# Spreading one modulation pair's one-column products over the k steps of a projection block

## The chip, the cores and the metric

The kernel runs on one core of a Trainium2 chip. The metric is the time of one execution on the device, in microseconds (us); lower is better.

## The reference

Two transformer blocks of one family run one after the other on 512 latent tokens and 256 context tokens of width 1024. What bears on this case is the first layer of the first block. From two condition vectors it makes six modulation vectors each, it norms and modulates the tokens, and it projects them to the inputs of four mixers:

```python
m = jnp.dot(jax.nn.silu(cond), w_mod) + b_mod          # 1024 -> 6 * 1024, for c and for c_ctx
h = modulate(rms_norm(x, norm1_g[l]), sh1, sc1)
q, k, v, u_pool, a_conv, b_conv = jnp.split(h @ w_in[l], SPLITS, axis=-1)
q = apply_rope(rms_norm(q.reshape(...), q_g)); k = apply_rope(rms_norm(k.reshape(...), k_g))
u = a_conv * jax.nn.sigmoid(b_conv)                     # 31 taps, then a layer norm over 256 channels
y = silu(layer_norm(depthwise_conv(u) + dw_b, ln_g, ln_b))
```

Attention, a pooling mixer, the output projection and a gated feed-forward follow. The second layer and the second block are of the same kind.

## The kernel before, in words

It is one program of hand-ordered instruction streams, one for each engine, that meet at semaphores. Activations lie with channels on the partitions and 768 tokens along the free axis. Weights are split into a high and a low part, so that each product of a weight tile with the activations is three matrix products: high with high, high with low, low with high. SyncE (SP) loads raw weights, ScalarE (ACT) writes `w_hi`, and GpSimd (POOL) or VectorE (DVE) writes `w_lo` = raw minus `w_hi`. Work is numbered in blocks `n` of mostly 256 output channels; two PSUM slots and two weight slots alternate. `gemm_done` counts the blocks that TensorE (PE) has finished, `lo_ready` the blocks whose `w_lo` is written, `psum_free` the evictions.

**The first layer's input projection** is ten blocks, b = 0 to 9. Blocks 0 and 1 make the convolution's input, 2 and 3 the pool's, 4 to 7 the queries and keys. Blocks 8 and 9 make the values with tokens on the partitions (`products_nat`): six token tiles of eight k steps each, 48 k steps of three products with 256 columns (line 2998). Between the k steps of block 8 stand small products that belong elsewhere, by the table `key_sums`: step number 0 to 11 each carries one product of the third group of head sums (the squares' sums over a head, two columns, line 3054), 12 to 23 one product of the convolution's sums of squares (one column, line 3108), 24 to 28 none, 29 to 40 one product of the fourth group of head sums, 41 to 47 none. The last of these four groups opens a chain: ACT takes the root (`roots(3)`, line 2113), DVE inverts it (`inverse(3)`, line 2590) and rotates the last keys (`rotate(3)`, lines 2596 to 2598), then multiplies the convolution's result (line 2660, semaphore `c_yn`), and PE's turn of the first key root (`turn_root(4)`, line 3128), which stands between the first and the second token tile of block 9, waits for that. Before it, at block 8's end, PE turns the convolution's root (`conv_root_turned`, line 760), which waits for the root of the fourth head sums.

**Modulation pairs.** A pair is 512 columns of `w_mod`, two rings of 256. DVE multiplies each weight row by the condition and accumulates (`pair_steps`, line 2496, 16 steps for a pair with both conditions), once for the latents in `mod_w` and once for the context in `mod_ctx`. PE then sums over the partitions with eight one-column products (`pair_sum`, line 2846), four blocks of 128 columns for each of the two conditions. The eight results are copied out of PSUM into `modc` (`pair_save`), which raises `mod_saved` by two. `pair_in_block` says behind which block's products a pair's sums stand. The pair of this case is (0, 6), the seventh of the first layer; its sums stand behind block 7. Its place in PSUM is shared in time with the convolution's sums and the fourth head sums, so these wait for `mod_saved`. SP loads the next pair's weights, (0, 7), only after `mod_saved` of (0, 6), and its queue then holds the swap of the last keys for `rotate(3)` (`load_swap`, line 635).

On DVE the order around block 7 is: convolution taps, four steps of pair (0, 6), the convolution's centring (line 2641, semaphore `c_yc`), the other twelve steps, `w_lo` of block 8 (`own_lo(8)`, line 2615), then the inverses and rotations. On ACT it is: `w_hi` of block 9 (line 1929) once block 7 is done, the save of the pair, block 7's squares and copy out of PSUM (lines 2207 and 2210), the root of the third head sums, the convolution's root (line 2236). `late_pair` is a semaphore that PE raises for a pair with sums in the middle of a block of the output projection.

## Time and profile before

| what | value |
|---|---|
| median of 3 runs | 2481.96 us (2480.01 to 2485.34) |
| profiled execution, its own time | 2481.36 us |
| its span in the profile | 2479.6 us |
| mean granted clock of TensorE | 0.982 |
| PE busy | 2393.6 us, 97% of the span |
| DVE, ACT, POOL busy | 1342.5, 818.2, 848.1 us |
| chain that ended last | PE 85%, DVE 10%, ACT 3% |
| queue of SP's loads | 238.41 MB, 31.6% of the 16 engines |

The span runs from the first to the last instruction seen; the execution's own time has 1.8 us more around it. A granted clock of 1.00 is TensorE's upper level, 2.4 GHz, and 0.50 its lower, 1.2 GHz. A matrix product's duration in a row of the timeline contains its way through the array, so that rows overlap; the pace is read from the starts. In a timeline a small f32 product appears as two rows merged into "x2".

### The profile page before, as it was taken

To read this page: it belongs to the slowest core of one execution; us is meant where nothing else is said; L and a number is where in the kernel's file an instruction comes from. 1 tells how busy PE (TensorE), PEld (TensorE's weight loads), DVE (VectorE), ACT (ScalarE), POOL (GpSimd) and SP (SyncE) were. 2 spreads that over 40 slices of the span, in tenths; PEclk is the share of its full clock that TensorE was granted. 3 is DMA by queue.
4 is the path that set the end of the run, shared out by engine and by line. 5 is a ranking of instruction groups with operands and counts; after the bars stand their busy time and mean duration, and the time that the engine had idled before them with its cause. 6 is when DMAs were issued, how large, how long until landed. Compare 5 with 4: busy or idle time off the path is not lost.

```text
span 2479.6 us, 31918 instructions
## 1 busy us (share of the span) xinstructions
PE 2393.6 (97%) x13433; PEld 2015.6 (81%) x13433; DVE 1342.5 (54%) x1823; ACT 818.2 (33%) x1195; POOL 848.1 (34%) x615
## 2 busy tenths in 40 slices
PE   7999889999999999998899999999999989999998
PEld 3889778888888888788788778778988678887877
DVE  3986677645543543697767755655563445211114
ACT  2322672321211112435742222235353454222223
POOL 1005103234333333205034554544453003444452
PEclk9997899999999999999999999999999999999999
DMA  8332112324342442223033545632113102233231
GB/s 259 119 102 87 35 35 70 101 95 120 113 141 90 138 131 89 73 86 104 1 103 106 166 146 168 196 102 85 52 35 102 34 1 69 82 99 100 83 96 68
DMA packets 309231, 240.58 MB, mean 97 GB/s; under 512 B 10692, under 2 KB 304831, under 8 KB 309087
## 3 DMA queue, kind: packets, MB, share of 16 engines
q1 hardware_dynamic: 308674, 238.41, 31.6%
q8 instruction: 106, 1.74, 0.3%
q14 instruction: 37, 0.30, 0.0%
q10 hardware_dynamic: 414, 0.13, 0.0%
HBM read 232.22 MB, written 2.10 MB: 95 GB/s over the span
## 4 chain that ended last, share of the span: by engine, by line
PE 85%; DVE 10%; ACT 3%; issue 1%; POOL 1%; DMA 1%; SPq 0%; DVEq 0%; ACTq 0%
PE ps L2893 54%; PE ps L2933 6%; PE ps L1339 5%; PE ps L2998 3%; PE ps L1098 2%; PE ps L1359 1%; DVE mod_w L2496 1%; DVE h_lo L2400 1%; PE ps L835 1%; PE ps L753 1%; PE ps L2811 1%; DVE small L1223 1%; DVE xg L2415 1%; POOL w_lo L1816 1%; PE ps L808 1%
## 5 line engine op out<-in xcount | busy, mean ns | idle before, releaser
L1816 POOL TENSOR_TENSOR w_lo<-raw,w_hi 128x512 fp32r<-128x512 f32 (+1 forms) x488 | 694.8, 1453 | 1260.1 <-ACT w_hi L1929 1260.1
L2893 PE MATMUL ps<-h_hi,w_hi 128*128 128x512 f32 (+1 forms) x1704 | 549.7, 368 | 3.3 <-DVE h_lo L2400 1.5
L2893 PE MATMUL ps<-h_hi,w_lo 128*128 128x512 f32 (+1 forms) x1704 | 541.5, 363 | 0.0
L2893 PE MATMUL ps<-h_lo,w_hi 128*128 128x512 f32 (+1 forms) x1704 | 541.2, 363 | 0.0
L1929 ACT ACTIVATE w_hi<-raw 128x2048 fp32r<-128x2048 f32 (+4 forms) x162 | 259.1, 1599 | 431.7 <-PE ps L2893 317.3
L2893 PEld LDWEIGHTS ps<-h_hi,w_hi 128*128 128x128 f32 x1704 | 287.0, 188 | 60.2 <-POOL w_lo L1816 3.6
L2893 PEld LDWEIGHTS ps<-h_hi,w_lo 128*128 128x128 f32 x1704 | 286.9, 188 | 56.0
L2893 PEld LDWEIGHTS ps<-h_lo,w_hi 128*128 128x128 f32 x1704 | 287.0, 188 | 54.8 <-issue 0.2
L2278 ACT ACTIVATE xg<-ps 128x512 f32<-128x512 f32 (+1 forms) x66 | 44.2, 670 | 636.0 <-PE ps L2893 388.0
L2496 DVE SCALAR_TENSOR_TENSOR mod_w<-mod_w,cond 128x512 f32<-128x512 f32 x217 | 224.2, 1033 | 3.4
L2893 PE MATMUL ps<-hid_hi,w_hi 128*128 128x512 f32 x632 | 210.0, 371 | 0.0
L2893 PE MATMUL ps<-hid_lo,w_hi 128*128 128x512 f32 x632 | 209.0, 370 | 0.0
L2893 PE MATMUL ps<-hid_hi,w_lo 128*128 128x512 f32 x632 | 208.8, 369 | 0.0
L2526 DVE SCALAR_TENSOR_TENSOR x<-ps,modc,x 128x512 f32<-128x512 f32 (+1 forms) x132 | 83.0, 680 | 182.5 <-PE ps L2893 182.5
L2760 DVE TENSOR_TENSOR sq<-xg,ps 128x512 f32<-128x512 f32 (+1 forms) x66 | 51.0, 773 | 237.4 <-ACT xg L2278 237.3
L2763 DVE TENSOR_TENSOR hid_lo<-sq,hid_hi 128x512 fp32r<-128x512 f32 (+1 forms) x66 | 88.0, 1333 | 76.9 <-ACT hid_hi L2282 76.9
L2893 PEld LDWEIGHTS ps<-hid_hi,w_lo 128*128 128x128 f32 x632 | 108.8, 189 | 22.2
L2893 PEld LDWEIGHTS ps<-hid_lo,w_hi 128*128 128x128 f32 x632 | 108.8, 189 | 21.9
L2893 PEld LDWEIGHTS ps<-hid_hi,w_hi 128*128 128x128 f32 x632 | 108.9, 189 | 21.7
L1260 DVE SCALAR_TENSOR_TENSOR conv_acc<-u_conv,col_b,conv_acc 128x783 f32<-128x783 f32 (+1 forms) x120 | 107.2, 893 | 3.9
L2496 DVE SCALAR_TENSOR_TENSOR mod_ctx<-mod_w,cond,mod_ctx 128x512 f32<-128x512 f32 x105 | 102.3, 975 | 0.0
L2933 PE MATMUL ps<-h_hi,w_hi 128*128 128x256 f32 (+1 forms) x288 | 86.7, 301 | 1.6 <-DVE h_lo L2400 1.6
(424 smaller groups left out, 4079.6 us busy)
## 6 DMA issues: line engine op xcount, KB each, us to landing
mod_w<-in_w_mod SPq DMA_DIRECT2D x72, 1024.0 KB, 8.2
raw<-in_w_ffn_in SPq DMA_DIRECT2D x88, 512.0 KB, 5.2
raw<-in_w_in SPq DMA_DIRECT2D x54, 512.0 KB, 4.9
raw<-in_w_ffn_out SPq DMA_DIRECT2D x48, 384.0 KB, 3.7
raw<-in_w_out SPq DMA_DIRECT2D x24, 512.0 KB, 4.7
raw<-in_w_gate SPq DMA_DIRECT2D x22, 512.0 KB, 4.0
raw<-in_w_up SPq DMA_DIRECT2D x22, 512.0 KB, 5.3
raw<-in_w_down SPq DMA_DIRECT2D x24, 384.0 KB, 3.4
```

The source lines that it names most:

```text
L1098: ins = pe.matmul(ps[:, PV2_AT:PV2_AT + 256], values(us[u]["k0"] // P + k, us[u]["h"]), probs_t[:, k, 256 * (j % 2):256 * (j % 2) + 256], ...
L1260: ins = dve.scalar_tensor_tensor(acc, frm, w, acc, ALU.mult, ALU.add)
L1339: ins = pe.matmul(ps[:, at:at + tw], weight, v[:, k, t0:t0 + tw], start=(k == 0 and r == 0), stop=(k == KD - 1 and r == 2))
L1816: ins = pool.tensor_tensor(lo[:, at:end], raw[:, s, at:end], hi[:, at:end].bitcast(F32), ALU.subtract)
L1929: ins = act.activation(to[:, at], raw[:, n % 2, at], ACT.Copy)
L2496: ins = dve.scalar_tensor_tensor(to, w, by, to if step >= chains else mod_bias[:, :, :], ALU.mult, ALU.add)
L2526: ins = dve.scalar_tensor_tensor(xt, ps[:, at:at + tw], modc[:, l % 2, chunk + 2 * b + t, c:c + 1], xt, ALU.mult, ALU.add)
L2760: dve.tensor_tensor(ffn_tile(ffn_h[:, s, 0:T], n, T), ffn_tile(ffn_sg[:, s, 0:T], n, T), ffn_columns(n, 1, T), ALU.mult).then_inc(psum_fre ...
L2763: dve.tensor_tensor(hid_lo[:, i, 0:T], ffn_h[:, s, 0:T], hid_hi[:, i, 0:T].bitcast(F32), ALU.subtract).then_inc(f_lo, 1)
L2893: ins = pe.matmul(ps[0:m, at:at + tw], weight(part, k, cols), v[:, held[k] if held else k, t0:t0 + tw], start=(at_k == 0 and j == 0 and no ...
L2933: ins = pe.matmul(ps[:, at:at + tw], w[:, k, P * tile:P * tile + P], v[:, held[k] if held else k, t0:t0 + tw], start=(at_k == 0 and j == 0 ...
L2998: ins = pe.matmul(ps[:, first + width * t:first + width * (t + 1)], v[:, k, rows], w[:, k, :], start=(k == 0 and j == 0), stop=(k == KD - ...
```

## The change

The eight one-column products of pair (0, 6) no longer stand behind block 7. They go one by one into k steps 12 to 19 of block 8, in their old order and with the old operands. The convolution's sums of squares move from steps 12 to 23 to steps 20 to 31, the fourth head sums from 29 to 40 to steps 35 to 46; of the free steps in between there are three instead of five, and behind the last head sum one instead of seven. ACT saves the pair after the root of the third head sums instead of ahead of block 7's eviction, and waits for `late_pair` there. The later reader of `late_pair` waits for 2 instead of 1. Block 7 ends with its own last product, and the wait for `c_yc` behind it is gone (the third head sums already wait for it). The second layer keeps its steps but for the fourth head sums, which begin three free steps behind the convolution's sums instead of five.

```diff
@@ ACT
-                        pair_save(lambda to, frm: act.activation(to, frm, ACT.Copy), n)
+                        if n != base_in[0] + 7:
+                            pair_save(lambda to, frm: act.activation(to, frm, ACT.Copy), n)
...
                         if b == 7:
                             roots(2)
+                            if l == 0:
+                                act.wait_ge(late_pair, 1)
+                                pair_save(lambda to, frm: act.activation(to, frm, ACT.Copy), n)
@@ DVE
                 if pair:
-                    dve.wait_ge(late_pair, 1)
+                    dve.wait_ge(late_pair, 2)
@@ PE
+            def pair_product(m, at, number):
+
+                ring, e, part = number // 4, number // 2 % 2, number % 2
+                if number == 0:
+                    pe.wait_ge(mod_mul, pair_ops[pair_at[m] + 1])
+                ins = pe.matmul(ps[:, at + number:at + number + 1], mod_part(ring, part, True)[:, P * e:P * e + P], ones[:, 0:1],
+                                start=True, stop=True)
+                if number == 7:
+                    ins.then_inc(late_pair, 1)
...
-                if n not in pair_in_block:
+                if n not in pair_in_block or n == base_in[0] + 7:
                     return None
...
                         number, conv, key = KD * t + k, 2 * T // P, 2 * TOK // P
+                        pair = key if l else key + 8
                         if number < key:
                             head_sum(2, number)
-                        elif number < key + conv:
-                            conv_square_sum(number - key)
-                        elif number >= key + conv + 5:
-                            head_sum(3, number - key - conv - 5)
+                        elif number < pair:
+                            pair_product((0, 6), pair_columns(base_in[0] + 7), number - key)
+                        elif number < pair + conv:
+                            conv_square_sum(number - pair)
+                        elif number >= pair + conv + 3:
+                            head_sum(3, number - pair - conv - 3)
...
-                            pair = then
-
-                            def pair_after_conv():
-
-                                pe.wait_ge(c_yc, 2 * l + 2)
-                                return pair()
-
                             products(n, KD, in_width(l, b), spans(TOK if b >= 6 else T), h_hi, h_lo, kr,
-                                     pair_after_conv if then and b == 7 else then, None, in_at, None,
+                                     then, None, in_at, None,
```

The first place is PE at the seam of blocks 7 and 8 (`mod_w` and `mod_ctx` hold the pair's sums, `w_hi`, `w_lo` the weights, `h_hi`, `h_lo` the activations, `qk_sq` the squares of the queries and keys). Before:

```order
779 L2893 MATMUL ps<-h_hi,w_lo 128x256
780 L2846 MATMUL ps<-const,mod_w 128x1 [waits mod_mul,c_yc]
781 L2846 MATMUL ps<-const,mod_ctx 128x1
...
787 L2846 MATMUL ps<-const,mod_ctx 128x1
788 L2998 MATMUL ps<-w_hi,h_hi 128x256 [waits psum_free0,lo_ready]
789 L2998 MATMUL ps<-w_hi,h_lo 128x256
790 L2998 MATMUL ps<-w_lo,h_hi 128x256
791 L3054 MATMUL ps<-const,qk_sq 128x2 [waits p_std,c_yc,p_sq]
```

And with the change:

```order
779 L2907 MATMUL ps<-h_hi,w_lo 128x256
780 L3012 MATMUL ps<-w_hi,h_hi 128x256 [waits psum_free0,lo_ready]
781 L3012 MATMUL ps<-w_hi,h_lo 128x256
782 L3012 MATMUL ps<-w_lo,h_hi 128x256
783 L3068 MATMUL ps<-const,qk_sq 128x2 [waits p_std,c_yc,p_sq]
```

The eight products are gone from the seam. Block 8's first product still waits for `lo_ready`.

The second place is PE at the end of block 8 and the start of block 9 (`v_nat` holds the squares of the fourth group, and the convolution's root that line 760 turns). Before, seven k steps follow the last head sum:

```order
946 L3054 MATMUL ps<-const,v_nat 128x2
947 L2998 MATMUL ps<-w_hi,h_hi 128x256
948 L2998 MATMUL ps<-w_hi,h_lo 128x256
...
967 L2998 MATMUL ps<-w_lo,h_hi 128x256
968 L760 MATMUL ps<-const,v_nat 128x128 [waits p_std,c_spread]
```

With the change one k step follows it:

```order
964 L3068 MATMUL ps<-const,v_nat 128x2
965 L3012 MATMUL ps<-w_hi,h_hi 128x256
966 L3012 MATMUL ps<-w_hi,h_lo 128x256
967 L3012 MATMUL ps<-w_lo,h_hi 128x256
968 L760 MATMUL ps<-const,v_nat 128x128 [waits p_std,c_spread]
```

The last head sum, and with it the root that `p_std` counts, stands six k steps nearer to what waits for it.

The third place is ACT after block 7 (`modc` is the save of the pair, `n_root` the convolution's root). Before:

```order
93 L1929 ACTIVATE w_hi<-raw 128x2048 [waits w_landed1,gemm_done]
94 L2182 ACTIVATE modc<-ps 128x8
95 L2207 ACTIVATE v_nat<-ps 128x2x512
98 L2210 ACTIVATE qk<-ps,col_b 128x2x256
99 L2113 ACTIVATE qk_root<-ps,const 128x24 [waits p_ss]
100 L2236 ACTIVATE n_root<-ps,const 128x6 [waits c_ss]
```

With the change:

```order
93 L1929 ACTIVATE w_hi<-raw 128x2048 [waits w_landed1,gemm_done]
94 L2208 ACTIVATE v_nat<-ps 128x2x512
97 L2211 ACTIVATE qk<-ps,col_b 128x2x256
98 L2113 ACTIVATE qk_root<-ps,const 128x24 [waits p_ss]
99 L2236 ACTIVATE modc<-ps 128x8 [waits late_pair]
100 L2240 ACTIVATE n_root<-ps,const 128x6 [waits c_ss]
```

The save has moved behind block 7's eviction and the third head sums' root. No instruction moves on DVE, POOL or SP.

## Rows read from the trace of the kernel before

**Rows 1.** Windows of core 0: busy us of each engine, granted clock, DMA.
```profile
core 0: us, PE busy (x) PEld busy (x) DVE busy (x) ACT busy (x) POOL busy (x), PEclk, DMA share, GB/s
195.00:198.00 3.00, 2.92 (x17) 2.27 (x16) 3.00 (x6) 0.00 (x0) 0.00 (x0) 1.00 0.00 0
198.00:201.50 3.50, 1.92 (x16) 1.86 (x16) 3.50 (x4) 0.01 (x1) 2.03 (x1) 1.00 0.00 0
202.50:226.50 24.00, 24.00 (x114) 24.00 (x114) 14.16 (x9) 4.24 (x7) 22.38 (x22) 0.50 0.67 220
226.50:229.00 2.50, 2.50 (x14) 2.50 (x14) 1.62 (x3) 1.11 (x2) 2.11 (x6) 0.50 0.04 15
229.50:239.00 9.50, 9.50 (x86) 9.50 (x85) 3.97 (x5) 2.20 (x4) 5.50 (x5) 1.00 0.01 3
```

**Rows 2.** Timeline of PE, seam of blocks 7 and 8 (start us, us, what, idle before).
```profile
197.41 0.51 PE L2893 MATMUL ps<-h_hi,w_lo 128*128 128x512 f32 x2
199.54 0.35 PE L2846 MATMUL ps<-const,mod_w 128*128 128x1 f32 x2 [1.61 <-DVE mod_w L2496]
...
201.65 0.39 PE L2998 MATMUL ps<-w_hi,h_hi 128*128 128x256 f32 x1 [0.19 <-DVE w_lo L2615]
...
202.37 0.56 PE L2998 MATMUL ps<-w_hi,h_hi 128*128 128x256 f32 x1
```

**Rows 3.** Timeline of DVE at the same place.
```profile
191.36 0.74 DVE L2496 SCALAR_TENSOR_TENSOR mod_ctx<-mod_w,cond,mod_ctx 128x512 f32<-128x512 f32 x1
...
199.30 2.29 DVE L2615 TENSOR_TENSOR w_lo<-raw,w_hi 128x2048 fp32r<-128x2048 f32 x1
```

**Rows 4.** Timeline of PE, starts of the first three k steps without a small product.
```profile
226.91 0.56 PE L2998 MATMUL ps<-w_hi,h_hi 128*128 128x256 f32 x1
...
227.69 0.41 PE L2998 MATMUL ps<-w_hi,h_hi 128*128 128x256 f32 x1
...
228.33 0.41 PE L2998 MATMUL ps<-w_hi,h_hi 128*128 128x256 f32 x1
```

**Rows 5.** Timeline of PE, end of block 8 and first turn in block 9.
```profile
236.04 0.36 PE L2998 MATMUL ps<-w_hi,h_hi 128*128 128x256 f32 x1
...
236.61 0.36 PE L2998 MATMUL ps<-w_hi,h_hi 128*128 128x256 f32 x1
...
239.08 0.82 PE L760 MATMUL ps<-const,v_nat 128*128 128x128 f32 x6
...
242.87 0.85 PE L3128 MATMUL ps<-const,qk_sq 128*128 128x128 f32 x6 [0.15 <-DVE conv_acc L2660]
```

**Rows 6.** Timeline of DVE, the chain behind the fourth head sums.
```profile
237.10 0.30 DVE L2590 RECIPROCAL qk_root<-qk_root 128x24 f32<-128x24 f32 x1 [5.49 <-ACT qk_root L2113]
...
240.78 1.94 DVE L2660 TENSOR_TENSOR conv_acc<-conv_acc,ps 128x512 f32<-128x512 f32 x4
```

**Rows 7.** Timeline of ACT.
```profile
203.31 0.16 ACT L2182 ACTIVATE modc<-ps 128x8 f32<-128x8 f32 x1
...
227.08 0.27 ACT L2236 ACTIVATE n_root<-ps,const 128x6 f32<-128x6 f32 x1 [12.52 <-PE ps L3108]
```

**Rows 8.** Timeline of SP's queue.
```profile
211.61 1.13 SPq L603 DMA_DIRECT2D mod_w<-in_w_mod  x2
...
216.60 1.26 SPq L635 DMA_DIRECT2D qk_swap<-qk  x2
```

**Rows 9.** Line 635, 200 to 260 us: landing times of its four transfers.
```profile
DMA to landing us min/median/max: 2.4/4.4/7.5
```

**Rows 10.** Timeline of DVE, the same chain in the second layer.
```profile
1144.46 1.29 DVE L2660 TENSOR_TENSOR conv_acc<-conv_acc,ps 128x512 f32<-128x512 f32 x2 [0.21 <-PE ps L760]
```

**Rows 11.** Timeline of PE, another wait for DVE, in the second layer's feed-forward.
```profile
1646.97 1.12 PE L2859 MATMUL ps<-const,mod_w 128*128 128x128 f32 x4 [3.70 <-DVE mod_w L2496]
```

**Rows 12.** Windows of core 0 around that wait.
```profile
1643.30:1645.90 2.60, 0.00 (x0) 0.00 (x0) 2.43 (x4) 0.07 (x1) 0.00 (x0) 1.00 0.00 0
1646.00:1649.30 3.30, 2.33 (x8) 2.05 (x9) 1.43 (x4) 1.18 (x2) 0.00 (x0) 0.50 0.00 0
```

## The prediction

> **What bounds the kernel now.** I read the windows with the granted clock first, because TensorE is busy 97% of the span and nearly everything hangs on its pace. From 195 to 198 us the clock is 1.00. From 202.5 us on it is 0.50, although PE is busy in all of these 24 us, and only from 229.5 us is it 1.00 again [rows 1]. So block 8 runs for some 27 us at the lower of TensorE's two levels, 1.2 GHz, and that stretch begins right where the change sets in. Ahead of the fall PE did little: in the 3.5 us from 198 us it was busy for 1.92 us, and that with 16 rows of one column each [rows 1].
>
> The timeline of PE says why. Block 7's last products start at 197.41 us and end at 197.92. PE then waits 1.61 us for the last `mod_w` of the pair, runs the eight products from 199.54 us, waits 0.19 us more for `w_lo`, and starts block 8 at 201.65 us [rows 2]. The releaser of the second wait is what counts. On DVE nothing is idle here: the pair's last twelve steps run back to back from 191.36 us, and `w_lo` of block 8 follows at once, 199.30 + 2.29 = 201.59 us [rows 3]. **Block 8 can't begin before 201.6 us, whether or not PE has sums to do.** The convolution's `c_yc`, the other wait that the change drops, had been given when line 2496 went on at 191.36 us [rows 3], long before block 7's end.
>
> Third, the pace inside block 8. With a small product in it, a k step takes (226.91 - 202.37) / 23 = 1.067 us at the lower clock [rows 2, 4]; without one 228.33 - 227.69 = 0.64 us [rows 4]. At the upper clock they take 236.61 - 236.04 = 0.57 us and (239.08 - 236.61) / 7 = 0.35 us [rows 5]. A small product thus costs 0.43 us at the lower clock and 0.22 us at the upper one: it is a weight load and a pass of next to no columns.
>
> **The change part by part.** The sum is made against the profiled execution, 2481.36 us, which is 0.6 us under the median of the runs.
>
> Block 7's tail: eight products and the wait for the pair leave it. They lay wholly beside DVE's way to `w_lo`. Gain at the start of block 8: 201.65 - 201.59, or at most 0.06 us. I take 0. PE is now idle from 197.92 to 201.65 us, 3.7 us in one piece.
>
> What ACT gains there is early, but nobody waits for it: `w_hi` of block 9 and block 7's eviction move up by some 3.5 us (`gemm_done` came behind the sums). The `w_lo` of block 9 follows in DVE's own order behind other work, and the first operation behind `w_lo` of block 8 has all it needs already. I take 0.
>
> Does the clock still fall? In the stretch before it fell, PE had the same length of poor work as now, only with small products in 1.92 us of it. Another wait of this trace is nearly the case to come: idle for 3.70 us for `mod_w`, and the clock went from 1.00 to 0.50 during it [rows 11, 12]. So it falls again at about 202 us.
>
> Eight more k steps with a small product: 8 x 0.43 = 3.4 us at the lower clock. They shift the first free step from 226.91 us [rows 4] to 226.91 + 8 x 1.067 = 235.4 us.
>
> The clock's return: in 24 us with a small product in each step it did not come back. It came at about 229.4 us, when PE had run 2.5 us of nothing but 256-column products [rows 1]. There were five such k steps and the products of a sixth. Now there are three and a fourth's, 4 x 0.64 = 2.56 us, so it is close. I take the return at 239.2 us: later than the earliest that this would allow (235.4 + 2.5 = 237.9), since the cover is just long enough. By then the three free steps are over (237.5 us) and 1.7 / 1.067 = 1.6 of the twelve head sums' steps. The rest: 10.4 x 0.567 = 5.9 us, and the last step 0.35 us. Block 8 ends at 245.5 us instead of 239.08 [rows 5]: **+6.4 us**. With the earliest return it is +5.8 us.
>
> The tail behind block 8: the fourth head sums end at 236.61 us, and `turn_root(4)` starts at 242.87 us, 6.26 us later, after ACT's root, DVE's inverse at 237.10, the rotation, and the convolution's product from 240.78 us [rows 5, 6]. None of this runs at PE's clock. Before, seven k steps, the turn of line 760 and block 9's first tile covered all but 0.15 us of it. Now six k steps of cover are gone. The turn starts 6.26 - 0.35 = 5.9 us behind block 8's end, where it was 242.87 - 239.08 = 3.8 us: **+2.1 us**. The other waits for that chain are on the same releasers, so attention moves with it, and nothing in it has a fixed time. Bounds: 0, if later idle time takes it up, to 2.3, with the root's latency counted at line 760 too.
>
> Small waits: the convolution's sums wait for the save of the pair. PE has 0.64 us of products between; the save itself took 0.16 us [rows 7]. I take 0, at most 0.3 us. The convolution's root took 0.27 us [rows 7] and now has 4 x 0.35 us of cover or more: 0.
>
> SP's queue: the load of pair (0, 7) was issued at 211.61 us [rows 8]; it now waits for the save, at about 202.37 + 19 x 1.067 + 0.6 = 223.3 us. Behind it stand the swap of the last keys, the pool's weights and the next raw weights. The swap comes 216.60 - 211.61 = 5 us after the pair's load [rows 8], so at 228.3 us, and lands at most 7.5 us later [rows 9], at 235.8 us. `rotate(3)` needs it behind the last head sums, at some 245 us. It is hidden. Were block 8 at the full clock, the same count would give 201.65 + 20 x 0.567 + 0.6 + 5 + 7.5 = 226.1 us against a need at 228 us: still hidden. Only without this cover would `rotate(3)` wait, and the swap would be what is late next.
>
> The second layer's fourth head sums come two steps earlier. There the convolution's product waits for line 760's turn [rows 10], not for the root, so this gives 0.
>
> Sum: 6.4 + 2.1 = +8.5 us, 2481.4 + 8.5 = 2489.9, or **2490.0 us**.
>
> One rule speaks against this reading of the clock. The Trainium skill (TensorE: Matmul & The Clock Gate, What's actually happening) has the clock set by how busy the engine has been, with the full clock soon after work is sustained. By that rule block 8 would be at full speed again shortly after it begins, and the change would give about 2474 us. The trace does not agree: busy for 24.00 of 24.00 us at 0.50 [rows 1]. So I go by the row: thinly filled steps don't bring the clock back.
>
> **The rivals.** First, *the clock isn't back before block 8 ends*, as the free stretch is 1.3 us shorter than the one that brought it. Then the twelve steps take 12 x 1.067 and the last 0.64 us: end at 237.5 + 13.4 = 251.0 us, +11.9, and the tail 1.8 (0.64 us of its 6.26 are covered): 2495.1 us. For it: the return took nearly all of what is left. Against it: 2.5 us did suffice once.
>
> Second, *a small loss*: the clock returns as early as before, at 229.4 us. Then 5.7 steps x 0.567, three free steps, twelve more and the last give 229.4 + 3.2 + 1.05 + 6.8 + 0.35 = 240.8 us, +1.7, with the tail +3.8: 2485.2 us. With later idle time taking up the tail it is under 2484. Against it: nothing in those 24 us brought the clock back.
>
> Third, **faster**: the clock doesn't fall at the seam. All of block 8 then runs at the upper level, 44 x 0.217 + 48 x 0.351 = 26.4 us, and ends at 228.1 us, 11.0 us earlier. With the tail's 2.1 us back: -8.9, 2472.5 us. It decides on one thing, the clock at 202.5 us. For it: the fall needed a poor stretch of just this length and might be marginal. Against it: that stretch has become poorer, and 3.70 us of idleness did it elsewhere [rows 11, 12]. If block 8 began at once at 198 us, that would bring this case too, but the end of `w_lo` in rows 3 excludes it.
>
> **How the numbers follow.** My forecast, the clock back in or right after the free steps, 2487 to 2493 us, gets 0.53. The clock back only after block 8, 2493 to 2498 us: 0.25. The small loss, 2482 to 2487 us: 0.14. The faster case 0.06, and 0.02 for one that ends a little under 2477 us. A difference of 0.2%, 5 us, is about what a measurement of this kernel can tell from no change. That makes 0.08 for faster, 0.14 for within, 0.78 for slower. The range, 2484.5 to 2497 us, takes in the first rival and the upper part of the small loss, and leaves out the faster case and both outer ends.
>
> **What would show it.** Right: PE idle for about 3.7 us before block 8's first product, which still starts at about 201.6 us behind line 2615; the clock at 0.50 from 202 us until 237 us or later; 32 k steps in a row with a small product; block 8's end near 245 us; `turn_root(4)` with an idle time of about 2 us for line 2660. Wrong: a clock of 1.00 at 205 us, or back before 232 us; a start of block 8 before 201 us; no idle time at `turn_root(4)`; `rotate(3)` waiting for its swap.

## The result and the profile after

| what | before | with the change |
|---|---|---|
| median | 2481.72 us, 7 runs | 2493.09 us, 7 runs |
| lowest and highest | 2479.79 to 2486.89 | 2486.55 to 2497.16 |
| ratio | 1 | 1.0040, 95% interval 1.0029 to 1.0050 |
| profiled execution | 2481.36 us, clock 0.982 | 2494.12 us, clock 0.978 |

The change costs 11.4 us by the medians, 7 to 12 by the interval. The forecast was 2490.0 us with 2484.5 to 2497.

The lines of TensorE's products have moved down by 13 to 17, those of DVE by 4, so that line 3012 is what line 2998 was, 3145 what 3128 was and 2664 what 2660 was. First the timeline of PE in the changed kernel, from the seam to the first root's turn (start us, us, what, idle before it):

```profile
199.30 0.51 PE L2907 MATMUL ps<-h_hi,w_lo 128*128 128x512 f32 x2
203.55 0.38 PE L3012 MATMUL ps<-w_hi,h_hi 128*128 128x256 f32 x1 [3.73 <-DVE w_lo L2619]
...
216.86 0.42 PE L2859 MATMUL ps<-const,mod_w 128*128 128x1 f32 x2
...
237.41 0.56 PE L3012 MATMUL ps<-w_hi,h_hi 128*128 128x256 f32 x1
...
240.11 0.42 PE L3068 MATMUL ps<-const,v_nat 128*128 128x2 f32 x2
...
247.75 0.85 PE L760 MATMUL ps<-const,v_nat 128*128 128x128 f32 x6
...
253.41 0.85 PE L3145 MATMUL ps<-const,qk_sq 128*128 128x128 f32 x6 [1.99 <-DVE conv_acc L2664]
```

The row at 216.86 us is the pair's first product, the one at 237.41 us the first step without a small product, the one at 240.11 us the first of the fourth head sums. Block 8 starts behind `w_lo`, as it did in [rows 2], after 3.73 us of one wait. It takes 247.75 - 203.55 = 44.20 us where it took 239.08 - 201.65 = 37.43 [rows 2, 5]. The turn stands 5.66 us behind its end and waits 1.99 us, against 3.79 and 0.15 [rows 5]. From block 8's first product to the turn that makes 49.86 us against 41.22, **8.6 us more**. Block 8's start is itself 1.9 us later in this execution. That is not the change: of the same code, another execution started it at 199.49 us (experiment 11).

The windows of the same stretch (busy us and instructions of PE, PEld, DVE, ACT, POOL, then the granted clock, DMA share and GB/s) answer to [rows 1]:

```profile
199.90:203.50 3.60, 0.00 (x0) 0.00 (x0) 3.60 (x5) 3.60 (x4) 2.13 (x1) 1.00 0.00 0
204.50:236.00 31.50, 31.50 (x148) 31.50 (x149) 14.07 (x9) 0.71 (x3) 27.72 (x32) 0.50 0.47 150
236.00:241.00 5.00, 5.00 (x26) 5.00 (x25) 3.08 (x4) 1.11 (x2) 0.00 (x0) 0.50 0.36 120
242.00:247.50 5.50, 5.50 (x51) 5.50 (x49) 0.00 (x0) 0.17 (x1) 0.00 (x0) 1.00 0.01 3
```

PE is idle for the whole of the seam, the clock falls behind it, stays at 1.2 GHz although PE is busy for every bit of the next 37 us, and returns at 241.5 us. Before, it was low for 27 us, from 202 to 229.5 us; now for 37.5.

DVE's timeline, to be held against [rows 3, 6]:

```profile
201.21 2.28 DVE L2619 TENSOR_TENSOR w_lo<-raw,w_hi 128x2048 fp32r<-128x2048 f32 x1
...
247.64 0.30 DVE L2594 RECIPROCAL qk_root<-qk_root 128x24 f32<-128x24 f32 x1 [6.07 <-ACT qk_root L2113]
...
251.33 1.94 DVE L2664 TENSOR_TENSOR conv_acc<-conv_acc,ps 128x512 f32<-128x512 f32 x4
```

And SP's queue, against [rows 8]:

```profile
225.05 0.99 SPq L603 DMA_DIRECT2D mod_w<-in_w_mod  x2
...
226.62 3.03 SPq L635 DMA_DIRECT2D qk_swap<-qk  x2
```

Before, the chain began at 237.10 us, 1.98 us ahead of block 8's end; now at 247.64, only 0.11 us ahead. The pair's load comes 13 us later than before and the swap 10, and nobody waits for them: `rotate(3)` follows on the inverse in DVE's own order.

Behind the turn the two profiles drift by some microseconds more. In the first layer's attention about 1.5 us of the difference is regained. In the second layer's attention the clock is low for 13.4 us (1183.5 to 1193.8 and 1245.0 to 1248.4 us) against 6.8 us (1174.9 to 1181.7 us), and the difference grows by 2.4 us. This growth does not repeat: in a second pair of profiles (experiments 10 and 11) the clock is low there for the same time in both kernels, 6.8 us, and the difference stays. The experiments return to what such stretches are worth.

### The profile page after: what moved, and what is told of

It reads as the page before. It is cut to its first block, busy times and chain, and to the rows that moved or that the text cites. A ratio compares the mean times of both kernels' runs of the same rounds, so it can differ in the third digit from the quotient of the medians.

```text
span 2492.3 us, 31918 instructions
## 1 busy us (share of the span) xinstructions
PE 2403.2 (96%) x13433; PEld 2024.7 (81%) x13433; DVE 1344.6 (54%) x1823; ACT 818.5 (33%) x1195; POOL 845.3 (34%) x615
## 4 chain that ended last, share of the span: by engine, by line
PE 85%; DVE 10%; ACT 3%; issue 1%; POOL 1%; DMA 1%; SPq 0%; DVEq 0%; ACTq 0%
PE ps L2907 54%; PE ps L2947 6%; PE ps L1339 5%; PE ps L3012 3%; PE ps L1098 2%; PE ps L1359 1%; DVE mod_w L2500 1%; DVE h_lo L2404 1%; PE ps L835 1%; PE ps L753 1%; PE ps L2815 1%; PE ps L1060 1%; DVE xg L2419 1%; POOL w_lo L1816 1%; PE ps L808 1%
```

## The experiments

Three questions: what the order alone costs (the head sums at the end), what the eight products cost, and what decides the clock's fall and return. All runs of a kernel are set against runs of the kernel before on the same chip. In the numbers, "the way to the turn" is the time from block 8's first product to the first root's turn: 41.22 us before, 49.86 with the change.

### 1. The fourth head sums six steps later, nothing else

```diff
-                        elif number >= key + conv + 5:
-                            head_sum(3, number - key - conv - 5)
+                        elif number >= key + conv + (5 if l else 11):
+                            head_sum(3, number - key - conv - (5 if l else 11))
```

The base is the kernel before.

> The kernel before, with the fourth head sums of the first layer six k steps later (steps 35 to 46) and nothing else moved. It prices the order alone. My theory (8.5 us in two parts, 6.4 in block 8 and 2.1 behind it): block 8 keeps its length of 37.4 us or loses up to 1 us, since its free stretch only grows; the turn of the first key root then waits about 2.0 us for the convolution's product, and the time is 2481.7 + 2 = 2483.7 us. Rival (the loss behind block 8 comes from the later load of the next pair and the queue behind it, not from the order): no idle time at that turn, 2481.7 us.

Measured: 2485.94 us (11 runs) against 2481.86 (25), ratio 1.0017 (1.0006 to 1.0028). PE at the end of block 8, from the timeline:

```profile
200.50 0.38 PE L2998 MATMUL ps<-w_hi,h_hi 128*128 128x256 f32 x1 [0.19 <-DVE w_lo L2615]
...
238.17 0.85 PE L760 MATMUL ps<-const,v_nat 128*128 128x128 f32 x6
...
243.83 0.85 PE L3128 MATMUL ps<-const,qk_sq 128*128 128x128 f32 x6 [1.99 <-DVE conv_acc L2660]
```

Block 8 takes 37.67 us, and the way to the turn is 43.33 us, 2.1 us more, with the same wait of 1.99 us as in the changed kernel. The term of the order is shown. The median is 4.1 us up, and the interval (1.5 to 6.9 us) holds 2.1. In the profiled execution the clock was low for 34.1 us between 250 and 376 us, where it had been low for 20.5; experiment 10 takes that up.

### 2. The eight products without their k steps

The base is the changed kernel. Its eight products share steps 2 to 9 with the third head sums, everything behind them goes back to its step of before, and the save goes ahead of the root.

```diff
                         if number < key:
+                            if l == 0 and 2 <= number < 10:
+                                pair_product((0, 6), pair_columns(base_in[0] + 7), number - 2)
                             head_sum(2, number)
-                        elif number < pair:
-                            pair_product((0, 6), pair_columns(base_in[0] + 7), number - key)
...
+                        elif number < key + conv:
+                            conv_square_sum(number - key)
+                        elif number >= key + conv + 5:
+                            head_sum(3, number - key - conv - 5)
```

> The changed kernel with the pair's eight products in k steps 2 to 9, which they share with third head sums, and the convolution's and fourth head sums at the steps they had before (five free steps, seven behind the last). It prices eight more small products in block 8 without the changed order. My theory: 8 x 0.43 = 3.4 us at the lower clock, block 8 takes 40.9 us, no wait of note at the first key root's turn, 2481.7 + 3.4 = 2485.1 us. Rival (the products cost little and the later return of the clock, by the short free stretch, is all of the 6.8 us): under 2483 us.

Measured: 2485.33 us (11 runs) against 2481.86, ratio 1.0014 (1.0005 to 1.0023). The timeline of PE:

```profile
200.25 0.39 PE L3012 MATMUL ps<-w_hi,h_hi 128*128 128x256 f32 x1 [3.73 <-DVE w_lo L2619]
...
241.13 0.81 PE L760 MATMUL ps<-const,v_nat 128*128 128x128 f32 x6
...
244.92 0.85 PE L3144 MATMUL ps<-const,qk_sq 128*128 128x128 f32 x6
```

And the windows:

```profile
202.00:231.00 29.00, 29.00 (x137) 29.00 (x137) 14.96 (x12) 1.57 (x4) 26.91 (x30) 0.50 0.57 184
232.00:241.00 9.00, 9.00 (x81) 9.00 (x80) 3.96 (x5) 2.15 (x4) 1.06 (x1) 1.00 0.01 3
```

Block 8 takes 40.88 us, 3.45 more than before, which is 8 x 0.43. The turn doesn't wait. So of the changed kernel's 6.8 us more in block 8, 3.4 are the products themselves, and the other 3.3 come with the new order of the steps.

### 3. PE kept at work in the seam

The base is the changed kernel. Seventeen products of 512 columns are added between blocks 7 and 8; their results are overwritten.

```diff
+                        if l == 0 and b == 8:
+                            pe.wait_ge(psum_free[0], n // 2)
+                            pe.wait_ge(hi_ready, n + 1)
+                            w_now = views(slot(n), KD, 256)[0]
+                            for i in range(17):
+                                pe.matmul(ps[:, 0:512], w_now[:, i % KD, 0:P], h_hi[:, i % KD, 0:512], start=True, stop=True)
```

> The changed kernel with 17 products of 512 columns in PE's idle time ahead of block 8 (3.7 us of work on valid data whose result block 8 overwrites; it adds to the computation and changes no output). My theory (the clock falls because PE does next to nothing for 3.7 us): the clock stays at 1.00 through block 8, which takes 26.4 us instead of 44.2, and the turn still waits 2 us: 2472.5 us, 20 us under the changed kernel. Rival (the thin k steps themselves bring the clock down, or the fall comes from elsewhere): the clock falls within block 8 and the time stays at 2485 us or more.

Measured: 2474.59 us (5 runs) against 2481.86, ratio 0.9968 (0.9954 to 0.9982). The windows:

```profile
196.00:200.00 4.00, 4.00 (x20) 3.12 (x18) 4.00 (x6) 3.77 (x4) 2.26 (x1) 1.00 0.00 0
200.00:226.90 26.90, 26.90 (x233) 26.61 (x232) 19.64 (x15) 3.07 (x8) 25.50 (x20) 1.00 0.61 199
```

The clock is never low in block 8, and it takes 26.9 us with exactly the small products that it has in the changed kernel. The seam's idleness is thus what brings the clock down here, and these small products by themselves do not: all 44 of them run at 1.00. Work that computes nothing makes the kernel 0.7% faster than the changed one (by the two ratios, 0.9968 / 1.0040 = 0.993), and 0.3% faster than the one before.

### 4. The seam filled with block 8's own work

The base is the changed kernel. Block 8's first two token tiles run their products with `w_hi` first, before `w_lo` is there; then PE waits for `w_lo` and adds the third product of each step. No arithmetic is added.

```diff
+                if lo_wait:
+                    for t in range(2):
+                        for k in range(KD):
...
+                            among(t, k)
+                    lo_wait()
+                    for t in range(2):
+                        for k in range(KD):
+                            pe.matmul(ps[:, first + width * t:first + width * (t + 1)], h_hi[:, k, rows], wl[:, k, :],
+                                      start=False, stop=(k == KD - 1), skip_group_check=True)
...
+                for t in range(2 if lo_wait else 0, tiles):
...
+                        elif l == 0 and b == 8:
+                            pe.wait_ge(psum_free[0], n // 2)
+                            pe.wait_ge(hi_ready, n + 1)
```

> The changed kernel with block 8 begun before its w_lo is there: for the first two token tiles all products with w_hi come first (each k step with its small product), then the wait for w_lo, then their products with w_lo; the other tiles as they were. The sums of two tiles are added up in another order. My theory: PE goes on at 197.9 us (in the time scale of the kernel before) without idle time, the clock stays at 1.00, block 8 ends at 224.3 us, 14.8 us earlier than before, the tail gives back 2.1: 2469 us. Rival (DVE's chain, or the swap's load, becomes the bound once PE is that early): block 9 or the turn waits for DVE by several us and the time is 2474 us or more.

Measured: 2474.18 us (7 runs) against 2481.86, ratio 0.9966 (0.9951 to 0.9981). One of the seven executions took 5076.2 us, and why it did was not looked into; the median of the other six is 2472.67 us. The windows:

```profile
196.50:223.00 26.50, 26.50 (x232) 26.37 (x231) 22.37 (x18) 6.66 (x11) 23.85 (x16) 1.00 0.56 179
223.00:231.00 8.00, 3.89 (x32) 3.52 (x31) 7.85 (x7) 3.08 (x5) 7.33 (x8) 1.00 0.24 75
232.00:235.00 3.00, 3.00 (x16) 3.00 (x15) 0.95 (x1) 3.00 (x5) 2.84 (x3) 0.50 0.00 0
```

Block 8 runs from 196.34 to 223.23 us, all at 1.00. But the turn comes only at 231.79 us, after 4.9 us of waiting, and the clock then falls for 3.5 us. DVE's timeline shows the new bound; its second operation here and the one of the same line and shape of an earlier group:

```profile
212.64 1.21 DVE L2601 TENSOR_TENSOR qk<-qk,rot 128x1024 f32<-128x1024 f32 x1
...
224.79 2.54 DVE L2601 TENSOR_TENSOR qk<-qk,rot 128x1024 f32<-128x1024 f32 x1
227.37 2.42 DVE L2602 TENSOR_TENSOR qk<-qk,qk_swap 128x1024 f32<-128x1024 f32 x1
229.71 1.93 DVE L2664 TENSOR_TENSOR conv_acc<-conv_acc,ps 128x512 f32<-128x512 f32 x4
```

The rival was right about the mechanism, with DVE's chain as the bound, and the gain fell 4 to 5 us short of my theory's 2469 us. In experiment 3 the clock is as high and block 8 as long, but the rotations take 1.16 to 1.23 us each and the way to the turn is 232.62 - 200.00 = 32.6 us; here it is 35.45. The two slow rotations stand beside GpSimd's wide sums; see the last section.

### 5 and 6. Two attempts to shorten the way to that turn

Both start from experiment 4. Experiment 5 puts the eight products two to a step (steps 12 to 15), so that the convolution's and the fourth head sums come four steps earlier. Experiment 6 lets them share steps 4 to 11 and puts the fourth head sums two to a step (27 to 32).

```diff
-                        pair = key if l else key + 8
+                        pair = key if l else key + 4
...
-                            pair_product((0, 6), pair_columns(base_in[0] + 7), number - key)
+                            for i in range(2):
+                                pair_product((0, 6), pair_columns(base_in[0] + 7), 2 * (number - key) + i)
```

> The run with block 8 begun before its w_lo is there, with the pair's products two to a k step (steps 12 to 15), so that the convolution's sums stand in steps 16 to 27 and the fourth head sums in 31 to 42. My theory (after the clock, the next bound is DVE's chain behind the fourth head sums, 4.9 us late at the turn): the chain starts 4 x 0.35 = 1.4 us earlier, the wait at the turn falls from 4.9 to 3.5 us or less, and the time from 2474.2 to about 2472.5 us. Rival (DVE's chain is held up by GpSimd's work beside it rather than by its start): the wait stays near 4.9 us and the time near 2474.

Measured: 2474.83 us (6 runs) against 2484.60 (17), ratio 0.9963 (0.9951 to 0.9975). Block 8 runs at 1.00 from 199.50 to 225.97 us, and the way to the turn is 34.06 us instead of experiment 4's 35.45. So the 1.4 us came as expected, but the turn still waits 3.95 us, where I had 3.5 or less: the rotation waited 0.95 us for its swap and again stood beside GpSimd. The median shows no gain over experiment 4.

```diff
                             head_sum(2, number)
+                            if l == 0 and number >= 4:
+                                pair_product((0, 6), pair_columns(base_in[0] + 7), number - 4)
...
+                        elif l == 0 and number >= key + conv + 3:
+                            for i in range(2):
+                                head_sum(3, 2 * (number - key - conv - 3) + i)
```

> As the run with block 8 begun before its w_lo, but the pair's products share k steps 4 to 11 with third head sums, the convolution's sums stand in 12 to 23, and the fourth head sums go two to a step in 27 to 32, so that 15 free steps cover the chain behind them. My theory: the clock stays at 1.00, the root of the fourth head sums comes some 5 us earlier, DVE goes through without idle time, and the turn waits under 1 us: about 2468 us. Rival (two small products to a step leave PE so thin that the clock falls): block 8 gets 3 us or more longer and the time is 2472 or more.

Measured: 2474.93 us (6 runs), ratio 0.9961 (0.9947 to 0.9975). The windows:

```profile
196.30:203.50 7.20, 7.20 (x66) 7.20 (x65) 7.20 (x7) 4.99 (x6) 5.47 (x2) 1.00 0.00 0
204.00:210.50 6.50, 6.49 (x30) 6.50 (x31) 6.46 (x3) 0.00 (x0) 6.34 (x3) 0.50 0.18 62
```

Here the clock falls in the midst of block 8, at 203.8 us, with PE busy all the time and no wait since the block began. The rival was right: block 8 takes 226.27 - 196.23 = 30.0 us, 3.1 more than in experiment 4, and the way to the turn is 35.6 us, no shorter than there. The turn waits 1.91 us. So an idle seam is one way to lose the clock and not the only one. What ran ahead of this fall were steps of two 256-column products with a two-column and a one-column product behind them; in experiment 4, with one small product in each of these steps, it did not fall. DVE's timeline shows the swap being late, as the prediction had it for the case without cover:

```profile
223.16 1.74 DVE L2600 TENSOR_TENSOR qk_swap<-qk_swap,rot 128x1024 f32<-128x1024 f32 x1 [1.49 <-DMA qk_swap<-qk]
```

Neither is better than experiment 4 by more than the intervals can tell.

### 7. Three free steps instead of five

The base is the kernel before.

```diff
-                        elif number >= key + conv + 5:
-                            head_sum(3, number - key - conv - 5)
+                        elif number >= key + conv + (5 if l else 3):
+                            head_sum(3, number - key - conv - (5 if l else 3))
```

> The kernel before, with the fourth head sums of the first layer two k steps earlier (steps 27 to 38), so that three free steps stand ahead of them instead of five and nine behind. No product is added. It isolates the shorter free stretch. My theory (five free steps brought the clock back 2.5 us into them, three give 2.56 us, so the return is late or fails in some executions): the clock is back 1 to 6 us later than 2.5 us into the free stretch, block 8 takes 38 to 41 us instead of 37.4, no wait at the turn: 2483 to 2485 us. Rival (three free steps are as good as five, the return depends on something else): block 8 takes 37.4 us, 2481.9 us.

Measured: 2481.77 us (11 runs) against 2484.60 (17), ratio 0.9992 (0.9982 to 1.0002). Block 8 takes 37.44 us, the clock is back at 228.9 us, and the turn at 241.60 us doesn't wait. My theory, that a free stretch of three steps delays the return, falls. PE's timeline around the return; the first row is the first free step, the second the first of the fourth head sums:

```profile
225.55 0.56 PE L2998 MATMUL ps<-w_hi,h_hi 128*128 128x256 f32 x1
...
228.25 0.42 PE L3054 MATMUL ps<-const,v_nat 128*128 128x2 f32 x2
228.53 0.53 PE L2998 MATMUL ps<-w_hi,h_hi 128*128 128x256 f32 x1
228.89 0.29 PE L2998 MATMUL ps<-w_hi,h_lo 128*128 128x256 f32 x1
```

The return came behind the three steps, 3.3 us after the first of them began and with the first head sum already done. That is within what other runs show: with five free steps it took 2.5 us in the first profile of the kernel before and 3.3 us in the second (experiment 10), and with eleven 4.0 us in experiment 1. The distance from the first free step isn't fixed. What is the same in all four is how long the clock was low in block 8, 27.3 us.

### 8. Free steps early in block 8

The base is the kernel before. Steps 12 to 19 carry nothing; the sums behind them stand where the change has them.

```diff
+                        elif l == 0 and number < key + 8:
+                            return
+                        elif number < key + conv + (0 if l else 8):
+                            conv_square_sum(number - key - (0 if l else 8))
+                        elif number >= key + conv + (5 if l else 11):
+                            head_sum(3, number - key - conv - (5 if l else 11))
```

> The kernel before, its pair's products still behind block 7, but with the convolution's and the fourth head sums at the changed kernel's k steps (20 to 31 and 35 to 46), so that steps 12 to 19 are free: the changed kernel's order with the eight steps empty instead of filled. My theory (a small product in each step keeps the clock at its lower level, and the steps in front of the free stretch are what runs slowly): the clock comes back 2.5 to 6 us into the free steps, near 217 to 220 us, block 8 takes 32 to 34 us instead of 37.4 and 44.2, the turn waits 2 us: 2477.5 to 2480 us. Rival (the clock comes back a fixed time after its fall, or by the amount of work done, not by free steps): back at 229 us or later, block 8 at 37 us or more, and with the wait at the turn 2483.8 us.

Measured: 2478.39 us (12 runs) against 2483.37 (23), ratio 0.9982 (0.9971 to 0.9993). The windows:

```profile
200.00:212.00 12.00, 12.00 (x58) 12.00 (x58) 11.97 (x6) 4.49 (x6) 11.61 (x6) 0.50 0.30 100
213.00:216.50 3.50, 3.50 (x19) 3.50 (x18) 1.74 (x3) 0.00 (x0) 3.04 (x7) 0.50 1.04 340
217.50:232.00 14.50, 14.50 (x130) 14.50 (x130) 3.67 (x4) 1.11 (x2) 13.34 (x18) 1.00 0.48 155
```

After 12 steps with a small product the free ones begin, at 212.44 us, and the clock is back at 216.9 us: it is low for 17 us instead of 27. It then stays up through 24 steps with small products. Block 8 takes 32.82 us instead of 37.43. Of these 4.6 us only 2.2 arrive at the turn, which waits 2.54 us and comes 39.03 us behind block 8's start: the fourth head sums stand as late as in experiment 1. Inside block 8 the order is the changed kernel's without its eight products, which stand in the seam as before; the clock falls at either seam. **So the eight products in steps 12 to 19 cost 44.20 - 32.82 = 11.4 us there**: they also keep the clock down.

### 9. Five free steps early

As experiment 8, but with steps 12 to 16 free, the convolution's sums in 17 to 28 and the fourth head sums in 31 to 42.

```diff
+                        elif l == 0 and number < key + 5:
+                            return
+                        elif number < key + conv + (0 if l else 5):
+                            conv_square_sum(number - key - (0 if l else 5))
+                        elif number >= key + conv + (5 if l else 7):
+                            head_sum(3, number - key - conv - (5 if l else 7))
```

> The kernel before with its five free k steps at 12 to 16, between the third head sums and the convolution's sums (17 to 28), two free ones, and the fourth head sums in steps 31 to 42. The same small products in the same number of steps. My theory: the clock is back near 217 to 220 us instead of 229, block 8 takes 32 to 34 us, the chain behind loses two steps of cover, 0.6 us: 2476.5 to 2479 us. Rival (as in the run with eight free steps): 2482.5 us.

Measured: 2482.84 us (11 runs) against 2483.37 (23), ratio 0.9997 (0.9986 to 1.0008), so the expected 2476.5 to 2479 us did not come. Block 8 came as expected, 32.62 us with the clock low from 199.9 to 217.0. But the turn waited 2.41 us for a rotation that had grown to 1.90, 1.63 and 1.64 us beside GpSimd, the way to it was 38.67 us, only 2.6 less than before though block 8 is 4.8 shorter, and in the attention behind it the clock was low for 27.3 us instead of 20.5.

### 10 to 12. The same kernels profiled again

Without any edit: the kernel before, the changed kernel, and experiment 9.

> The kernel before, unchanged, profiled once more. Theory: which of the thin stretches of the first layer's attention fall to the lower clock differs from one execution to the next, so the sum of the low stretches between 255 and 370 us will differ from the 20.5 us of its first profile by at least 3 us, or their places will; block 8 itself (201 to 239 us, low until 229 or 230) stays as it was. Rival: the places are fixed by the kernel's own schedule; then the same three stretches (from 270.4, 304.5 and 359.1 us) return within 1 us.

> The changed kernel, unchanged, profiled once more. Theory: block 8 takes 43 to 44.5 us again, with the clock back somewhere between 237.5 and 242 us, and the first root's turn about 5.7 us behind its end, while the low stretches of the attention behind it lie elsewhere than in the first profile. Rival: all of it returns in the same places within 1 us, and the time is then fixed by the schedule alone.

> The kernel before with the free steps at 12 to 16, as in the earlier run of this edit, profiled once more. Theory: the 27.3 us of lower clock that its first profile shows in the attention (255 to 370 us) was that execution's draw; another one shows 20 to 27 us in other places. Rival: this schedule brings the attention into a rhythm in which more stretches fall, so the same five stretches return, 27 us in all.

The same views as before, of the same code in another execution:

| kernel | execution, us | block 8 starts | block 8 | way to the turn | low clock, 250 to 376 us |
|---|---|---|---|---|---|
| before | 2481.36 | 201.65 | 37.43 | 41.22 | 20.5 |
| before again | 2484.69 | 200.16 | 37.46 | 41.25 | 27.3 |
| changed | 2494.12 | 203.55 | 44.20 | 49.86 | 20.5 |
| changed again | 2489.86 | 199.49 | 44.23 | 49.89 | 27.3 |
| experiment 9 | 2482.37 | 199.69 | 32.62 | 38.67 | 27.3 |
| experiment 9 again | 2480.27 | 200.38 | 31.07 | 37.35 | 23.9 |

One stretch of the attention shows it best; first in the kernel before, then in the same kernel again (windows):

```profile
310.50:317.50 7.00, 7.00 (x51) 6.12 (x52) 3.93 (x10) 3.05 (x13) 0.00 (x0) 1.00 0.22 64
```

```profile
269.50:279.50 10.00, 10.00 (x39) 8.64 (x38) 6.66 (x12) 4.54 (x10) 0.00 (x0) 0.50 0.27 91
303.50:306.50 3.00, 3.00 (x9) 2.38 (x8) 1.14 (x2) 0.00 (x0) 0.00 (x0) 0.50 0.00 0
310.50:317.50 7.00, 7.00 (x29) 5.92 (x30) 2.63 (x6) 2.02 (x7) 0.00 (x0) 0.53 0.29 91
```

The way to the turn repeats within 0.03 us in both kernels of the comparison, though not in experiment 9, where the clock came back at 215.5 us instead of 217.0 the second time. The changed kernel's clock was back at 237.25 us the second time, a little ahead of the 237.5 to 242 us expected; counted from the first free step that is 3.7 us, against 4.1 the first time. It was low for 37.5 us in both.

What differs from execution to execution is when block 8 starts, by up to 4 us, and how long the clock is low in the attention, 20 to 27 us. For the kernel before, its first two low stretches returned at nearly the same offset from block 8's start and one more was added, so the rival of fixed places holds in part. In the changed kernel the first low stretch began at the same offset too (75.4 and 75.3 us), but lasted 13.7 us the second time instead of 3.4, and those behind it came 3 us later.

What this is worth can be read at the first product of the next norm (line 753), behind the attention. From block 8's start to there the kernel before took 168.1 and 171.5 us, the changed one 175.3 and 178.3: 3.3 and 3.0 us more where the clock was low for 6.8 us more. Between the two kernels it is 7.2 us in the first pair and 6.8 in the second, so of the 8.6 us at the turn the attention gives back 1.5 to 1.8 in either pair. The block-8 comparison is free of the spread. The whole executions are not: the two pairs differ by 12.8 and 5.2 us, of which 1.9 and -0.7 were there before block 8 began. So a median of a few executions can carry some 2 us of this, which is the size of what experiments 1 and 9 were off by. That it accounts for just those two is likely and not shown.

## Why the prediction was right, point by point

**The start of block 8 gains nothing.** Right. PE waits 3.73 us in one piece for `w_lo`, where I had 3.7, and the wait before block 8 was as long in both profiled executions of the change. In experiment 4, which takes that wait away, the block starts at 196.34 us.

**The clock falls at the seam.** Right, and experiment 3 shows the cause: with PE at work in the seam the same block 8 runs at 1.00. In experiment 4 it does so with its own products in the seam.

**Eight k steps with a small product more, 3.4 us.** Right: 3.45 us in experiment 2.

**The clock's return at 239.2 us.** The size was about right and the reason wrong, so it is in part luck that the point was hit so closely. It came at 241.5 us in an execution whose block 8 started 1.9 us later, so 0.4 us behind my point, and block 8 took 6.8 us more where I had 6.4. But I had put the lateness on the shorter free stretch, "three and a fourth's", and experiment 7 shows three free steps bringing the clock back about as early as five. What counts is when the free steps come, not how many there are: the change moves them from steps 24 to 28 to steps 32 to 34. Eight steps' own products, which had run behind the return, now run ahead of it, 8 x (0.64 - 0.35) = 2.3 us by the paces of [rows 4, 5]. With the small products' 3.4 us that is 5.7. Of the missing 1.1 us most is again low clock: it lasts 37.5 us against 27.3, in both pairs of profiles, which is 10.2 us more where eight steps account for 8 x 1.067 = 8.5. The other 1.7 us at little over half the pace cost some 0.8 us. Why they are added stays open. The 2.5 us behind the first free step [rows 1, 4] on which the term was built were one execution's: the second profile of the kernel before has 3.3, the two of the change 4.1 and 3.7, so that distance is no constant. Experiment 8 is the other side of it: free steps at 12 to 19, and 4.6 us are won.

**The tail, 2.1 us.** Right: 5.66 - 3.79 = 1.9 us, in the changed kernel and in experiment 1, with the wait on the releaser that the prediction named.

**Small waits, SP's queue, the second layer: 0.** Right in the changed kernel. The pair's load came at 225.05 us and the swap at 226.62, where I had 223.3 and 228.3 (the swap followed the load by 1.6 us, not by 5), and `rotate(3)` didn't wait. In the kernels without this cover it did, by 0.95 and 1.49 us (experiments 5 and 6).

**The sum, 8.5 us** for the way to the turn: 8.6 measured, in two executions. The median is 11.4 us up, at 2493.09 us: just past the band of 2487 to 2493 us that I had given to my own mechanism and at the foot of the one for the clock coming back only after block 8, which the trace excludes. The rest, under 3 us, has no place in these runs. The first layer's attention isn't it, as it gives back 1.5 to 1.8 us of the 8.6 in both pairs of profiles; the interval (7 to 12 us) holds the 8.6. I had written that nothing behind the turn has a fixed time and that attention moves with it; it moves, but it isn't rigid.

**The page's rule.** The Trainium skill (TensorE: Matmul & The Clock Gate, What's actually happening) would have had block 8 back at full clock soon after its start. The changed kernel was busy for 31.50 of 31.50 us at 0.50, so going by the row was right. The same section also says, of a kernel's start, that one kernel's share of slow products can vary from run to run. The trace shows such a variation in the midst of a kernel: the clock was low for 20.5 and 27.3 us of the attention in two executions of the kernel before.

**The rivals.** The clock back only after block 8 did not come, nor did the return at 229.4 us. The faster case was no outcome of this edit, but its price was good: I had -8.9 us with the clock up, and experiment 3 gave -7.3.

## What to carry to other kernels

Before moving small products out of an idle seam into a dense stretch, ask what the seam was waiting for: here another engine's weights ended the wait, so nothing was gained there, and each small product then cost 0.43 us on the bound engine. Placed ahead of the free steps, where they also put off the clock's return, the eight cost 11.4 us against leaving their steps empty. If TensorE idles shortly before a block whose steps hold small products, the block can run at the lower clock for as long as they last, as here for 37.5 us; it pays to fill the wait with the block's own work that needs nothing late (-0.3%, experiment 4), or at least to place plain steps early (-0.2%, experiment 8). But look at what then waits: the same idea in experiment 9 won 4.8 us in block 8, 2.6 at the turn and nothing that the medians can tell. Judge such a change by the stretch it touches, from a common start to a common end, and by the medians only after that: the stretch repeated within 0.03 us, single executions of one kernel differ by 10 us.

## What the runs showed of the hardware that was not expected

**A clock that depends on what the engine's busy time consists of.** In experiment 6 it fell with PE busy for 7.20 of 7.20 us ahead of the fall and 6.49 of 6.50 behind it, and with no wait since the block began. In the changed kernel it stayed low for 37 us of full busy time and came back only behind plain steps. Yet in experiment 3, coming from a full clock, all 44 steps with the same small products kept it up. So the same mixture held whichever level it found, in these runs.

**Rotations that take twice as long.** DVE's product of two 128x1024 tiles took 1.21 us at 212.64 us of experiment 4 and 2.54 us at 224.79. GpSimd's timeline in the same kernel tells the two apart:

```profile
209.36 9.67 POOL L1884 TENSOR_TENSOR u_conv<-u_conv,const 64x8 f32<-64x8 f32 x8
...
223.87 2.38 POOL L1871 TENSOR_TENSOR u_conv<-u_pool 128x799 f32<-128x799 f32 x1
226.33 2.37 POOL L1871 TENSOR_TENSOR u_conv<-u_conv 128x797 f32<-128x797 f32 x1
```

And in the changed kernel, where DVE had nothing to do at the time:

```profile
224.41 1.52 POOL L1871 TENSOR_TENSOR u_conv<-u_pool 128x799 f32<-128x799 f32 x1
```

GpSimd was busy in both cases. Beside its eight-column operations DVE kept its 1.21 us, and it was GpSimd that paid: eight of them took 9.67 us there and 2.12 us in the changed kernel from 227.60 us, with DVE idle. Beside its 799-column ones both engines slowed, DVE by 1.3 us and GpSimd by 0.9. The times fit the two taking turns, by this estimate: GpSimd's first wide sum ends at 226.25 us, and 1.21 us behind that is 227.46, where the rotation ended at 227.33. The Trainium skill (GPSIMD Engine Reference, 1. Specifications) says that GpSimd and VectorE share their access to SBUF and contend when a VectorE instruction has two SBUF inputs; these rows agree, and give the size. It is part of why winning time in block 8 brought less at the turn: earlier, the rotation meets work that it had missed. Against the 3.59 us of the kernel before, the three operations of this rotation took 2.9, 2.1 and 3.1 us more in experiments 4 to 6 and 1.6 in experiment 9. In experiments 5 and 6 the late swap comes on top. In experiment 8 it was only 0.6 us, and the lost cover did the rest.
